# Hybrid decoder trunk on eight cores: the embedding gate by tanh instead of sigmoid, a scan's scratch moved out of a norm's buffer, the first loads in another turn, and the squares of tiles 1 and 2 on VectorE

## What is computed

```python
gate = jax.nn.sigmoid(rmsnorm(h, norm_ple[i]) @ ple_w_gate[i])
h = h + gate * (p[i] @ ple_w_proj[i])
```

## Time and profile before

| | |
|---|---|
| median of 3 runs | 1787.09 us (1786.84 to 1788.02) |
| profiled execution, own time | 1787.4 us |
| its span on the core shown (core 0) | 1785.8 us |
| spans of all cores | 1776.7 to 1785.8 us |
| TensorE busy | 1691.7 us (95%), 11096 matmuls |
| VectorE, ScalarE, GpSimd busy | 1223.3, 1015.9, 446.6 us |
| activation table loads on ScalarE | 156, 200.1 us |

### The profile page before, as it was taken

One profiled execution on the slowest core, in us unless ns is written; L12 is line 12 of the kernel. 1 busy time (PEld: TensorE's weight loads), 2 busy tenths in 40 slices (PEclk: granted clock), 3 DMA queues, 4 the chain that ended last, 5 costly groups with the idle time before them and its releaser, 6 DMA issues.

```text
span 1785.8 us, 35476 instructions; the slowest of 8 cores (1776.7 to 1785.8 us)
## 1 busy us (share of the span) xinstructions
PE 1691.7 (95%) x11096; PEld 1076.0 (60%) x11096; DVE 1223.3 (69%) x2544; ACT 1015.9 (57%) x1995; POOL 446.6 (25%) x897
## 2 busy tenths in 40 slices
PE   4799999799999999999899999999999999999985
PEld 2466656466666666666555556666666666666654
DVE  2566656997767676776657666787676776677666
ACT  3877779654444444479944432854434444449984
POOL 1533333311111111112354222201111111112343
PEclk8899999999999999999999999999999999999997
DMA  8800030045031221200272000403140404030023
GB/s 173 172 27 1 1 64 14 1 85 103 13 59 28 46 46 27 48 13 1 58 137 53 1 1 1 85 3 60 37 72 1 72 1 72 1 60 1 1 75 130
DMA packets 21675, 82.44 MB, mean 46 GB/s; under 512 B 1778, under 2 KB 12850, under 8 KB 15604
## 3 DMA queue, kind: packets, MB, share of 16 engines
q0 software_dynamic: 8224, 59.16, 18.7%
q1 hardware_dynamic: 12292, 19.80, 3.3%
q10 hardware_dynamic: 976, 1.21, 0.2%
HBM read 129.29 MB, written 10.03 MB: 78 GB/s over the span
## 4 chain that ended last, share of the span: by engine, by line
PE 79%; ACT 7%; issue 5%; DVE 5%; DMA 2%; POOL 1%; DVEq 0%; ACTq 0%; POOLq 0%; SPq 0%
PE PS L582 79%; ACT SB L530 4%; DVE SB L566 3%; ACT L530 2%; DVE SB L541 1%; DMA SB<-xT 1%; POOL SB L541 1%; DMA SB<-lru_w_x_in 1%; ACT PS L530 1%; ACT SB L571 1%; POOL SB L557 0%; DVE SB L557 0%; DVE SB L1296 0%; DVE SB L970 0%; DVEq L293 0%
## 5 line engine op out<-in xcount | busy, mean ns | idle before, releaser
L582 PE MATMUL PS<-SB 128*128 128x352 bf16 (+6 forms) x11096 | 1691.7, 314 | 87.3 <-ACT SB L530 40.9
L582 PEld LDWEIGHTS PS<-SB 128*128 128x128 bf16 x11096 | 1076.0, 98 | 702.8 <-issue 131.1
L541 DVE TENSOR_TENSOR SB<-SB,PS 128x352 bf16<-128x352 f32 (+6 forms) x1112 | 532.1, 512 | 164.9 <-PE PS L582 106.0
L566 DVE SCALAR_TENSOR_TENSOR SB<-SB 128x352 f32<-128x352 f32 (+1 forms) x720 | 380.8, 548 | 218.1 <-ACT SB L571 200.2
L530 ACT ACTIVATE SB<-PS,SB 128x352 f32<-128x352 f32 (+1 forms) x432 | 257.0, 616 | 366.4 <-PE PS L582 353.2
L530 ACT ACTIVATE SB<-SB 128x352 f32<-128x352 f32 (+6 forms) x678 | 314.7, 501 | 174.5 <-DVE SB L566 134.0
L573 POOL COPY SB<-SB 128x2 f32<-128x2 f32 (+2 forms) x472 | 150.7, 323 | 778.8 <-ACT SB L571 651.6
L541 POOL TENSOR_TENSOR SB<-SB 128x352 f32<-128x352 f32 (+6 forms) x242 | 230.2, 965 | 269.0 <-DVE SB L541 153.0
L566 DVE SCALAR_TENSOR_TENSOR SB<-SB,PS 128x352 bf16<-128x352 f32 (+6 forms) x344 | 174.2, 565 | 111.4 <-ACT PS L530 110.3
L530 ACT ACT_TABLE_LOAD x156 | 200.1, 1283 | 60.7 <-PE PS L582 48.5
L530 ACT ACTIVATE SB<-PS 128x352 f32<-128x352 f32 (+8 forms) x234 | 107.2, 472 | 125.9 <-PE PS L582 99.4
(11 more groups left out here) (26 smaller groups left out, 43.2 us busy)
## 6 DMA issues: line engine op xcount, KB each, us to landing
SB<-ffn_w_up POOLq DMA_DIRECT2D x24, 1024.0 KB, 11.3
SB<-ffn_w_down POOLq DMA_DIRECT2D x12, 1024.0 KB, 8.9
SB<-xT SPq DMA_DIRECT2D x10, 704.0 KB, 7.7
yT<-SB SPq DMA_DIRECT2D x10, 704.0 KB, 3.4
SB<-ple_w_gate POOLq DMA_DIRECT2D x2, 2048.0 KB, 14.6
SB<-gm_w_in POOLq DMA_DIRECT2D x2, 2048.0 KB, 16.6
SB<-pT POOLq DMA_DIRECT2D x2, 1056.0 KB, 14.3
SB<-lru_w_x_in POOLq DMA_DIRECT2D x4, 512.0 KB, 12.5
```

The lines of the kernel that those rows point to most:

```text
L541: emit(eng, lambda e: e.tensor_tensor(out=out.ap, in0=a.ap, in1=b.ap, op=op), R=[a, b], W=[out], cost=c)
L566: emit("dve", lambda e: e.scalar_tensor_tensor(out=out.ap, in0=a.ap, scalar=sa, in1=b.ap, op0=op0, op1=op1), R=rr, W=[out], cost=c)
L582: emit("pe", lambda e: e.matmul(ps.ap, lhsT=lhsT.ap, rhs=rhs.ap, start=start, stop=stop), R=[lhsT, rhs], W=[ps], cost=max(0.05, 0.000427 * ...
```

## The change

Four edits. The gate's sigmoid(z) is written as (1 + tanh(z/2))/2: the half is put into the projection weights by two VectorE operations a layer after they have landed, and the product is `(tanh + 1) * pp` in one instruction in place of the former product. The scratch `t16` leaves `r5`, and has a row for each channel block. The first loads have other turns and other loads to wait for. The squares of the norms of tiles 1 and 2 in the LRU stage go to VectorE (they were on ScalarE and GpSimd).

```diff
         xbuf_s = [r5([NSEQ, 7], BF16) for _ in range(2)]
-        t16 = r5([NSEQ], F32)
         xc = [T(mem, [TN], BF16, off=XN[4].off + i * TN * 2) for i in range(8)]
+        t16 = rl([8, NSEQ], F32)
...
         for q in range(4):
-            load("pool", lw_x.v(q), kp(w_lx_in[q], KC), K("lwx%d" % q), hblock(2, 4, 0, TN) if q == 0 else None)
-        load("pool", lw_a.all(), kp(w_la, KC), K("lwa"))
+            load("pool", lw_x.v(q), kp(w_lx_in[q], KC), K("lwx%d" % q), hblock(2, 4, 0, TN) if q == 1 else None)
+        load_x(1, 2, lw_x.v(1))
+        load("pool", lw_a.all(), kp(w_la, KC), K("lwa"), hblock(0, 8, TN, TN))
         load("pool", lw_i.all(), kp(w_lx, KC), K("lwi"))
-        load_x(1, 2, lw_x.v(1))
         for q in range(2):
-            load("pool", lw_g.v(q), kp(w_lg_in[q], KC), K("lwg%d" % q), hblock(0, 8, TN, TN) if q == 0 else None)
-        load_x(2, 2, lw_i.all())
+            load("pool", lw_g.v(q), kp(w_lg_in[q], KC), K("lwg%d" % q))
+        load_x(2, 2, lw_g.v(0))
         load("pool", lw_o.all(), kp(w_lout, KC), K("lwo"), hblock(0, 8, 2 * TN, TN))
-        load_x(3, 2, lw_g.v(1))
+        load_x(3, 2, lw_o.all())
...
                 load("pool", slot.pproj.all(), kp(w_pp[l], 2), K(slot.name + "d"))
+                for k in range(2):
+                    ts(slot.pproj.v(k), slot.pproj.v(k), 0.5, ALU.mult)
...
-                tt(t16.all(), a3, h0s.v(c), ALU.mult)
-                tt(b3, b3, t16.all(), ALU.add)
+                tt(t16.v(c), a3, h0s.v(c), ALU.mult)
+                tt(b3, b3, t16.v(c), ALU.add)
...
-        bg.append(("lru", lru_norm(1, "act")))
-        bg.append(("lru", lru_norm(2, "pool")))
+        bg.append(("lru", lru_norm(1, "dve")))
+        bg.append(("lru", lru_norm(2, "dve")))
...
-            act(th, ps, AF.Sigmoid)
-            tt(th, th, pp, ALU.mult)
+            act(th, ps, AF.Tanh, scale=0.5)
+            stt(th, th, 1.0, pp, ALU.add, ALU.mult)
```

## The result

| | before | after |
|---|---|---|
| median | 1787.32 us (1786.84 to 1788.02, 4 runs) | 1776.64 us (1776.02 to 1777.1, 4 runs) |
| ratio | | 0.994, 95% interval 0.9923 to 0.9957 |
| spans of the 8 cores, median | 1784.1 us | 1771.8 us |
| slowest core shown | core 0, 1785.8 us | core 6, 1774.5 us |

The change is worth 10.7 us. Forecast were 28, and 1776.64 lies just outside the range.

What follows compares the result with a forecast made beforehand. TensorE was taken as the bound, with 94.1 us idle plus half-clock loss to regain. Terms -12 - 3 - 5 - 7 - 2 = -29 us from 1787.4 gave 1758.4, stated as 1759; range 1746 to 1776.

Steps and rivals of the forecast that it cites:

- start: First stage, up to about 84 us: new load turns and squares on VectorE give -12 us (-3 to -18).
- scratch: Near 340 us: moving `t16` ends a wait for VectorE's memset, -3 us (0 to -6).
- gate 0: Embedding gate of layer 0: fewer ScalarE table loads cut TensorE's idle time, -5 us (-2 to -7.3).
- gate 1: Gate of layer 1: fewer ScalarE table loads cut TensorE's idle time, -7 us (-3 to -10).
- end: Final norms after the last gate matmul: the 352 norm of tile 3 comes ahead, -2 us (0 to -6).
- `lw_a` is issued there and lands 7.3 us later, at 35 to 36: First loads: `lw_a` goes out when x of tile 1 lands, at 28 us, and takes 7.3 us.
- ScalarE can pass at 58 to 62: First stage: Ln of tile 2 can run 6 us after its x lands at 52 to 56 us.
- x of tile 3 behind `lw_o`: First stage: this load has little cover before its squares fall due; uncovered it costs say 4 us.
- The rival of a held first stage: Rival, chance 0.05: ScalarE's Ln of tile 2 holds the first stage until its x lands; at 95, total 1799 us.
- Port contention: First stage: VectorE's squares still hold GpSimd up; relief 2.2 us in place of 6.2, sum 4 us higher.
- the table sets: ScalarE, whole program: table loads fall from 156 to 96, 77 us of ScalarE's time.
- the output product of tile 5 needs all scans: Near 340 us: with VectorE full, TensorE gets going about 3 us earlier, not 8.7.

Runs made afterwards that it cites:

- e13: Changed kernel with `lw_a` behind the second part of `lw_x`, `lw_g` behind x of tile 1, x of tile 2 behind `lw_i`: 1773.4 us.
- e15: e13 with x of tile 3 waiting for the second part of `lw_g`, not for `lw_o`: 1770.2 us.
- e4: Kernel before with only the squares of tiles 1 and 2 moved to VectorE: 1779.7 us.
- e1: Kernel before with the tanh gate edit alone: 1780.1 us.
- e5: Kernel before with two edits, squares of tiles 1 and 2 on VectorE and the tanh gate: 1769.4 us.
- e6: Changed kernel with the loads of before (squares, tanh gate and `t16` edits kept): 1769.7 us.
- e12: e5 with the first part of `lw_x` issued at once and the second waiting for x of tile 0: 1769.5 us.
- e14: e6 with the first part of `lw_x` issued at once and the second waiting for x of tile 0: 1769.9 us.
- e8: Changed kernel with `lw_a` no longer waiting for x of tile 1: 1783.0 us.

## Why the prediction was wrong

Medians over cores, us:

| term | forecast | measured | from |
|---|---|---|---|
| start | -12 (-3 to -18) | -1.7 | FFN 0 -4.3, less 2.6 |
| scratch | -3 | -2.6 | idle from 300 us, 10.4 to 7.8 |
| gate 0 | -5 | +2.3 (idle -4.1) | FFN 0 to FFN 1, mixer 1 included |
| gate 1 | -7 | -8.3 | -10.0, less the end |
| end | -2 | -1.7 | time left when two sums are to come, 22.0 to 20.3 (cores shown) |

**The start failed, and in its landings.** "`lw_a` is issued there and lands 7.3 us later, at 35 to 36": it is issued where GpSimd's list has it, behind the copies of seven `xb_group`s, at 34.6, and lands at 41.6. The prediction had quoted that list, and priced the transfer but not the place. The DMA engines were busy 0.79 of the first 84 us, so a pause of theirs moves every later landing: x of tile 2 came at 60.8. "ScalarE can pass at 58 to 62" failed twice, by that landing and because the sum of tile 2 stands 34 matmuls later in TensorE's list than with the old loads: 71.8. And x of tile 3 behind `lw_o` was priced at 4 and not counted; it holds the start only once the other two are mended, and then costs 5.7 at FFN 0 (e13 to e15). The rival of a held first stage was the right mechanism, with x of tile 2 at 60.8 and not at the 87 that would have turned the sign. What the sum called the start's gain is real, but belongs to the squares alone: 10.1 us in e4, against a list that spends 29.2 us from tanh to tanh, where 28 were forecast.

**Port contention** was weighed at 4 us. The squares of tile 1 take 3.62 us with GpSimd idle, those of tile 2 5.05 beside its work, and two products of GpSimd among them take 1.04 and 1.06 us in place of 0.77: together 2 us, and 10 came back all the same (e4). The means hide who waits. The eight squares of tile 2, shortest, median and longest in ns:

```profile
L541 DVE TENSOR_TENSOR SB<-SB x8: 509/541/1089, 60.8 to 65.3; 128x352 bf16<-128x352 f32 x8
```

Five of them take 0.51 to 0.57 us, as those of tile 1 do, and the three beside a product take 0.79, 1.09 and 1.09. The Trainium skill (SBUF — State Buffer, on the engine and DMA sides of SBUF) has the loser wait for a whole instruction. This trace nearly agrees for the products: the squares lost 1.4 us, and two products by themselves take 1.5. What the prediction had too high is the price: GpSimd had two products to do in that time, and VectorE bore most of the waiting.

**Gate 0** lost its idle time as forecast, and gained a fall of the clock in its place. Before, the clock stays at full (2.4 GHz) through waits of 1.74 and 1.88 us; after, one wait of 1.45 us, with single matmuls between products around it, is followed by about 6.6 us at half (1.2 GHz). Windows of before, and of the changed kernel behind it:

```profile
884.00:888.00 4.00, 2.60 (x18) 1.47 (x16) 0.52 (x1) 3.86 (x5) 0.51 (x1) 1.00 1.14 244
888.00:894.00 6.00, 3.37 (x21) 1.90 (x22) 4.46 (x10) 5.94 (x11) 1.85 (x2) 1.00 0.25 53
```

```profile
886.00:891.00 5.00, 3.01 (x18) 1.40 (x16) 2.40 (x6) 3.16 (x5) 1.84 (x3) 1.00 0.93 161
891.00:898.00 7.00, 6.66 (x21) 2.86 (x22) 3.32 (x7) 2.21 (x3) 1.25 (x2) 0.52 1.14 221
```

All kernels with the tanh gate have such a fall between 875 and 910 us on every core, and none with the sigmoid has one. From 880 to 905 us the clock is 0.86 on six cores of the changed kernel and 0.93 on two, a loss of 3.5 and 1.75 us against the 4.1 us of idle time gained. Why the shorter waits bring it and the longer ones don't stays open; no experiment here separates it. The prediction counted the clock at the start and forgot it in the gates.

The +2.3 us of the table is more than the gate, though. With the gate edit alone (e1) the stretch is 0.9 us shorter than before, 825.6: there the clock takes back most of the 4 us of idle time, not all. The rest of the +2.3 comes with further falls in mixer 1, near 950 us (3.4 us on seven cores, where before five lose 1.7 and three 3.4) and from 980 to 1100. The load, scratch and square edits by themselves lengthen the stretch by 2.2 to 3.1 us, with its lists unchanged.

**Right** were the table sets (96 loads, no load between tanh and gelu), gate 1, the end (from the last 128-column gate matmul to the end of the span 24.0 to 20.3 us on the cores shown, where 4 less were forecast) and the size of the scratch term. Of its two reasons one is seen. TensorE now waits there for the output product of tile 5, whose operands `gate_mult` makes on GpSimd, each behind a scan of VectorE. TensorE and GpSimd in the changed kernel:

```profile
334.84 0.45 PE L582 MATMUL PS<-SB 128*128 128x352 bf16 x1 [2.02 <-POOL SB L541]
337.89 0.45 PE L582 MATMUL PS<-SB 128*128 128x352 bf16 x1 [1.79 <-POOL SB L541]
```

```profile
333.25 2.25 POOL L541 TENSOR_TENSOR SB<-SB 128x352 bf16<-128x352 bf16 x2 [0.89 <-DVE SB L541]
336.39 2.16 POOL L541 TENSOR_TENSOR SB<-SB 128x352 bf16<-128x352 bf16 x2 [0.89 <-DVE SB L972]
```

So what the prediction called "the output product of tile 5 needs all scans" is what limits the gain. The norm's products on VectorE, the other reason, are not what TensorE waits for at these two places.

**The best version** can't be told: e5, e6, e12, e14 and e15 lie near 0.990 with intervals that overlap. e15 starts FFN 0 earliest, 14.5 us before the kernel before, and its median core in the profiled execution is the shortest, 1760.2 us; the mean over the cores of all its counted runs is 1761.8, beside 1762.1 in e6. Its slowest core takes 1769.0: there FFN 0 starts at 377.3, 4.3 after the median core, and FFN 0 to FFN 1 takes 832.0, by falls of the clock, where six of the others take 822.8 to 828.6. That keeps the 14.5 us from showing in full.

## What to carry to other kernels

When loads are put in another turn, follow two lists and not one: where each issue stands in its engine's queue, and where the work that needs the data stands in the consumer's; then look for a pause of the DMA engines, since in a stage where they are 0.7 to 0.8 busy it can delay what comes behind it. Try several edits made together one by one before trusting the sum: here one of four took back 7 us of 17. In a program on eight cores the slowest core sets the time, so a gain of idle time is only safe with the granted clock of all cores beside it.

## What was not expected of the hardware

- TensorE's clock falls to half while TensorE is full, in the mixer of layer 1 (between 980 and 1100 us), up to three times on a core at 1.7 us each; identical lists take 822.4 to 829.6 us on the cores of one execution (e12), by these falls and by those near 890 and 945 us, which also differ between its cores. In the 400 us of full load in either FFN no core of the kernel before or of the changed one has such a fall.
- A 704 KB half of x takes 9.7 us to land beside two weight parts, 16.5 beside four (e4), and 26.5 when 2 MB of `lw_g` are queued beside it as well (e8).
